# The last three experts of each layer: loads and products in the order gate, up, down of one expert

## What is computed

```python
def moe(h, router_w, router_b, w_gate, w_up, w_down):
    ...
    gates = jnp.sum(jax.nn.one_hot(idx, N_EXPERTS, dtype=jnp.float32) * w[..., None], axis=1)
    a = jnp.einsum("td,edf->tef", h, w_gate)
    u = jnp.einsum("td,edf->tef", h, w_up)
    z = jax.nn.silu(a) * u * gates[:, :, None].astype(h.dtype)
    return jnp.einsum("tef,efd->td", z, w_down)
```

```python
    h2 = rmsnorm(x, norm2_g) * (1 + scale2) + shift2
    x = x + gate2 * moe(h2.reshape(bsz * l, -1), router_w, router_b, w_gate, w_up, w_down).reshape(bsz, l, -1)
```

## Time and profile before

| | us |
|---|---|
| median of 3 runs | 1229.93 |
| lowest, highest | 1221.55, 1231.03 |
| profiled execution | 1229.87 |
| its span in the trace | 1228.2 |
| PE busy | 1109.6 (90%) |
| DVE busy | 558.6 (45%) |
| ACT busy | 355.9 (29%) |
| POOL busy | 234.7 (19%) |
| share of PE in the chain that ended last | 60% |
| share of DMA in that chain | 22% |

### The profile page before, as it was taken

The page is one execution under the profiler, slowest core; times in us unless marked ns, Lnnn a source line. Parts: engine busy times, 40 slices in busy tenths (PEclk is TensorE's granted clock), DMA queues, the critical chain, the costliest instruction groups (busy, mean ns, idle before and its releaser), DMA issues.

```text
span 1228.2 us, 18292 instructions
## 1 busy us (share of the span) xinstructions
PE 1109.6 (90%) x6948; PEld 520.5 (42%) x6948; DVE 558.6 (45%) x1342; ACT 355.9 (29%) x661; POOL 234.7 (19%) x339
## 2 busy tenths in 40 slices
PE   3999999899999987898899999998997999888886
PEld 1545556454443332333244655554544333232332
DVE  1275666743463332323265747666155433223327
ACT  2223445532323221221131424453223322221212
POOL 1222273411010111101020324541200011011100
PEclk9999889889989999999899998997998999899998
DMA  9939731656499999999790412046716799999995
GB/s 364 317 137 170 127 115 58 229 206 274 176 361 379 396 390 407 398 401 401 313 361 18 146 69 83 21 175 250 291 69 249 270 391 397 396 403 407 395 388 189
DMA packets 51214, 325.09 MB, mean 265 GB/s; under 512 B 6710, under 2 KB 7126, under 8 KB 32576
## 3 DMA queue, kind: packets, MB, share of 16 engines
q1 hardware_dynamic: 39296, 293.16, 61.1%
q0 software_dynamic: 10560, 26.17, 8.5%
q10 hardware_dynamic: 1280, 4.72, 0.9%
HBM read 316.15 MB, written 22.25 MB: 276 GB/s over the span
## 4 chain that ended last, share of the span: by engine, by line
PE 60%; DMA 22%; DVE 12%; issue 3%; ACT 2%; SPq 1%; DVEq 0%; ACTq 0%; POOLq 0%
PE ps L2216 19%; DMA ring<-moe_w_up 18%; PE ps L1828 14%; PE ps L1903 7%; PE ps L2106 7%; PE ps L1844 3%; DMA ring<-ada_w 3%; DVE attT L1318 2%; PE ps L1867 2%; PE ps L2000 2%; PE ps L2029 2%; DVE dbuf L1294 1%; PE ps L2205 1%; PE ps L1862 1%; DVE small L1427 1%
## 5 line engine op out<-in xcount | busy, mean ns | idle before, releaser
L2216 PE MATMUL ps<-ring,dbuf 128*32 128x512 f32 x2432 | 421.9, 605 | 35.0 <-DMA ring<-moe_w_up 23.5
L2216 PE MATMUL ps<-extra,dbuf 128*32 128x512 f32 x1312 | 248.9, 624 | 14.3 <-DMA ring<-moe_w_up 13.5
L2216 PEld LDWEIGHTS ps<-ring,dbuf 128*32 128x32 f32 x2432 | 115.3, 111 | 231.2 <-issue 220.6
L1828 PE MATMUL ps<-ring,extra 128*128 128x512 f32 (+1 forms) x384 | 150.6, 552 | 0.0
L1604 DVE COPY dbuf<-ps 128x256 f32<-128x256 f32 (+1 forms) x32 | 15.4, 483 | 212.3 <-PE ps L2205 212.3
L1903 PE MATMUL ps<-extra,ring 128*128 128x384 f32 x320 | 110.1, 503 | 0.0
L2216 PEld LDWEIGHTS ps<-extra,dbuf 128*32 128x32 f32 x1312 | 68.7, 114 | 89.5 <-issue 76.3
L866 POOL DMA_INDIRECT expert_rows<-big,lst x28 | 26.3, 940 | 409.6 <-DVE big L1626 205.2
L1828 PEld LDWEIGHTS ps<-ring,extra 128*128 128x128 f32 x384 | 74.3, 195 | 70.2 <-issue 66.7
L2106 PE MATMUL ps<-ring,extra 128*128 128x512 f32 x192 | 84.3, 594 | 3.0 <-DVE extra L1493 1.8
L1903 PEld LDWEIGHTS ps<-extra,ring 128*128 128x128 f32 x320 | 62.2, 197 | 42.7 <-issue 4.9
(11 more groups left out here) (310 smaller groups left out, 1452.9 us busy)
## 6 DMA issues: line engine op xcount, KB each, us to landing
extra<-moe_w_gate SPq DMA_DIRECT2D x32, 2048.0 KB, 17.3
ring<-moe_w_up SPq DMA_DIRECT2D x32, 2048.0 KB, 23.3
ring<-moe_w_down SPq DMA_DIRECT2D x30, 2048.0 KB, 22.3
ring<-ada_w SPq DMA_DIRECT2D x24, 2048.0 KB, 8.7
ring<-w_in SPq DMA_DIRECT2D x12, 2048.0 KB, 19.9
ring<-w_out SPq DMA_DIRECT2D x4, 2048.0 KB, 7.8
extra<-moe_w_down SPq DMA_DIRECT2D x2, 2048.0 KB, 15.9
skew_rows<-rpb_pad POOLq DMA_DIRECT2D x1, 3810.0 KB, 66.9
```

The costliest lines, as they stand in the source:

```text
L1828: ins = pe.matmul(out, a, b, start=(n == 0), stop=(n == len(pairs) - 1))
L2216: return pe.matmul(p[QT * g:QT * (g + 1), :], a, w, start=start, stop=stop, tile_position=(0, QT * g))
```

## The change

The last seven places of the load queue become down 13, gate 14, up 14, down 14, gate 15, up 15, down 15. On TensorE, experts 12 and 13 keep the old body; then `own_down(1)` runs the down product of 13 at once, and experts 14 and 15 (`alone=True`) run gate/up, and right behind it their own down product. `last_products` goes. On VectorE the scaling of expert 13's rows moves ahead of expert 14, the gate rows of 14 and 15 and the first `late_rows` move ahead of expert 15's product, and one `added` moves ahead of the second `late_rows`. The diagonal products run first, and the six `"cm"` products behind them; `keep_running(2)` goes. POOL's load of the final gain waits for the last gate/up product, since its slot now holds gate 14.

```diff
-            if q == 3 * NE - 1:
-                return "dn1", NE - 1
+            if q >= 3 * NE - 7:
+                return (("dn1", NE - 3), ("a", NE - 2), ("u", NE - 2), ("dn1", NE - 2), ("a", NE - 1), ("u", NE - 1), ("dn1", NE - 1))[q - 3 * NE + 7]
...
                 if l == L - 1:
+                    ready(pool, ("a", l), NE - 1)
                     pool.dma_start(fin, final_norm_g.partition_broadcast(P)).then_inc(d_fin, 16)
...
-                for e in range(EXP_PER_BODY):
-                    expert(NBODY - 1, e, next_=(e < EXP_PER_BODY - 1))
-                expert(NBODY, 0, last=True, next_=False)
+                expert(NBODY - 1, 0)
+                expert(NBODY - 1, 1)
+                products_out(NE - 3, SMALL)
+                for e in (2, 3):
+                    expert(NBODY - 1, e, next_=(e == 2), alone=True)
+                    products_out(NE - EXP_PER_BODY + e, SMALL)
+                act.activation(rneg[:, 0, :], eps, ACT.Sqrt)
...
-                for e in range(EXP_PER_BODY):
-                    expert(NBODY - 1, e, next_=(e < EXP_PER_BODY - 1))
+                expert(NBODY - 1, 0)
+                expert(NBODY - 1, 1)
+                rows_out(NBODY - 1, 1)
+                expert(NBODY - 1, 2, alone=True)
+                for j in range(LATE):
+                    gate_rows_of(NBODY - 1, EXP_PER_BODY - LATE + j, gate_rows[1], crossed=(j == 1))
                 if AHEAD[l]:
                     scales(l + 1, 0)
-                for j in range(LATE):
-                    gate_rows_of(NBODY - 1, EXP_PER_BODY - LATE + j, gate_rows[1], crossed=(j == 1))
                 late_rows(0)
+                expert(NBODY - 1, 3, next_=False, alone=True)
                 added(0, 0)
                 added(0, 1)
+                added(1, 0)
                 late_rows(1)
-                added(1, 0)
                 added(1, 1)
+                added(2, 0)
                 completed(0)
-                added(2, 0)
                 completed(1)
                 completed(2)
...
-                            if f == FC // 2 and not last and not next_:
-                                turn_products(es)
...
+                def own_down(es):
+
+                    e, blk = NE - EXP_PER_BODY + es, ("expert", l, queue_place("dn1", NE - EXP_PER_BODY + es))
+                    moved(pe, *product_of(l, NBODY - 1, es))
+                    turn("zt", e, [zb[0:CAP, f * P:(f + 1) * P] for f in range(FC)])
+                    pe.wait_ge(landed[SLOT_OF[blk]], 16 * NTH[blk])
+                    w = slot_of(SLOT_OF[blk]).rearrange("p (k n) -> p k n", k=FC)
+                    moved(pe, ("zt", l), e)
+                    job = (("dnz", l), 0) if e == NE - 1 else (("dn0", l), e)
+                    p = begin(pe, *job)
+                    for f in range(FC):
+                        for g in range(4):
+                            third, b = g % 2, g // 2
+                            ins = quarter(p, g, products_turned(SMALL)[:, f, QT * third:QT * (third + 1)], w[:, f, b * 512:(b + 1) * 512],
+                                          f == 0, f == FC - 1)
+                    fill(ins, *job)
...
-                for e in range(EXP_PER_BODY):
-                    expert(NBODY - 1, e, next_=(e < EXP_PER_BODY - 1))
-                expert(NBODY, 0, last=True, next_=False)
-                keep_running(2)
+                expert(NBODY - 1, 0)
+                expert(NBODY - 1, 1)
+                own_down(1)
+                for e in (2, 3):
+                    expert(NBODY - 1, e, next_=(e == 2), alone=True)
+                    own_down(e)
+                for n, (t, k) in enumerate(PE_PICKS):
+                    pe.wait_ge(d_yr[t][k], 16 * (l + 1))
+                    for b in range(2):
+                        pe.matmul(begin(pe, ("cm", l, t, b)), pick_diag[:, n, :], yr[k][:, t, b * 512:(b + 1) * 512], start=True, stop=False)
                 pe.wait_ge(s_fold, l + 1)
```

More of the change, by code:

```diff
@@ L1129, in expert @@
+                    if not first and not alone:
+                        products_out(e - 1, cap_of(i, es - 1))
                     if next_:
                         turned_out(e + 1, (es + 1) % 2, cap_of(i, es + 1))
-                    if not last and cap_of(i, es) == CAP:
+                    if cap_of(i, es) == CAP:
                         p = ready(act, ("u", l), use_of("u", i, es))
                         act.activation(by_chunk(sU)[0:2 * QT], in_rows(p)[2 * QT:P], ACT.Copy).then_inc(s_half, 1)
-                    if not first and next_ and cap_of(i, es - 1) == CAP:
+                    if not first and not alone and cap_of(i, es - 1) == CAP:
@@ L1626, in rows_out, with expert @@
                         release(dve, dve.tensor_tensor(y[0:SMALL, 512:D], p[SMALL:P], g[SMALL:P, 512:D], ALU.mult), ("dn0", l), e)
-                def expert(i, es, first=False, next_=True):
+                def expert(i, es, first=False, next_=True, alone=False):
                     e = i * EXP_PER_BODY + es
@@ L1652, in expert @@
                                                               op0=ALU.mult, op1=ALU.mult), ("u", l), n_u)
-                    if not first and next_:
+                    if not first and not alone:
                         rows_out(i, es - 1)
@@ L2216, in quarter, with expert @@
                     return pe.matmul(p[QT * g:QT * (g + 1), :], a, w, start=start, stop=stop, tile_position=(0, QT * g))
-                def expert(i, es, first=False, last=False, next_=True):
+                def expert(i, es, first=False, next_=True, alone=False):
                     e = i * EXP_PER_BODY + es
@@ L2250, in turn_products @@
                         turn("zt", i * EXP_PER_BODY + es, [zb[0:CAP, f * P:(f + 1) * P] for f in range(FC)])
-                    if not first and not last:
+                    if not first and not alone:
                         turn_products(es - 1)
@@ L2255, in expert @@
                         turn_rows(i, es + 1)
-                    if not last and large:
+                    if large:
                         n_u = use_of("u", i, es)
@@ L2277, in expert @@
                         fill(ins, *job)
-                    if not first and before_large:
+                    if not first and not alone and before_large:
                         n_dn = use_of("dn1", i, es - 1)
```

77 lines of the change are left out of this document (31 added, 46 removed).

## The result

| | before | after |
|---|---|---|
| median, us | 1229.95 (10 runs) | 1236.3 (10 runs, 1228.1 to 1238.75) |
| profiled execution, us | 1229.87 | 1236.45 |
| its span, us | 1228.2 | 1234.6 |
| PE busy | 1109.6 (90%) | 1100.3 (89%) |
| DVE busy | 558.6 (45%) | 557.7 (45%) |

The ratio of after to before is 1.0046, 95% interval 1.0024 to 1.0067: the change costs 5.7 us (3.0 to 8.2). The forecast was 3.1. The two profiled executions lie 6.6 us apart.

A forecast was written before the change was run, and what follows sets the result against it. The prediction took the in-order stream of expert weights, through the up-weight loads, to bound both expert parts. It summed 1229.87 us + 1.8 (first layer) + 1.3 (second) = 1233.0 us; this case's own range was 1226 to 1238.

The forecast's parts named there:

- Order of loads: Load queue, both layers: landing places are dealt out anew, so up weights of 14 and 15 land 5 us later.
- The stream did not catch up: Rival on weight loads: up weights of 14 and 15 land at their old times, 1222.6 us; chance 0.12.
- d13 costs nothing: TensorE: expert 13's down product, 3.62 us, fits into idle time before expert 14's up weights land; nothing lost.
- Clock of a14: TensorE, expert 14's gate/up product: 8.77 us taken, between 7.11 at full clock and 9.99; total 1231.5 to 1235.4 us.
- Own down product: TensorE, experts 14 and 15: 6.9 us from gate/up product's end to down product's end, the latter taking 3.62.
- The clock rival: TensorE's clock falls in the new bubbles: 3.6 us more per down product, four of them, 1247 us; chance 0.11.
- The sum: Expert part of each layer, up to x done: +1.8 us in the first layer, +1.3 us in the second.
- It reaches the end undiminished: After the first layer: its +1.8 us carries through, since TensorE's own work follows without waits for weights.
- VectorE's moved work: VectorE's end: some 5.8 us less behind expert 15's gated product; without it the end about 4.5 us later.
- Rows of 13 and reload: Store and reload of expert 13's rows: issued 11 us earlier, queued behind the last weights, landed by 1211; gain 0.24 us.
- the reload mixes with the weights: Rival: reload served beside the last weights, expert 15's up weights up to 5 us later per layer, 1242 us; chance 0.05.
- Diagonal products: TensorE's end, second layer: they run from 1212.1 to 1214.0, late-row products to 1219.3, with 0.6 us to spare.

The follow-up runs named there:

- e9: The changed kernel run once more without any edit; measured 1234.97 us, ratio 1.0043 to before.
- e1: The changed kernel with two unread filler matmuls between expert 15's gate/up product and the transposes of its products, in both layers; 1231.73 us, ratio 1.0007.
- e3: The changed kernel with the load order of before, keeping the new order of products; 1239.0 us, ratio 1.0119, from four runs.
- e10: The changed kernel with two unread filler matmuls ahead of expert 15's transposes, run a second time; 1232.2 us, ratio 1.0040.
- e6: The changed kernel with VectorE's gate rows, late rows and additions in the order of before; 1238.59 us, ratio 1.0083.
- e5: The changed kernel with the reload of stored rows held back until expert 15's gate/up product is done; 1246.8 us, ratio 1.0141.

## Why the prediction was right, and where its sizes were off

The sign and the mechanism were right: slower by a part of a per cent, because u14 and u15 land one place later and a bubble stands where the down product of before gave cover. The size was short: 3.1 us forecast, 5.7 (3.0 to 8.2) measured, so the forecast lies at the very edge of the interval. Two terms were short, d15's clock and u15's landing, and both on the same side. Step by step:

**Order of loads.** Second layer: the expert part starts 2.8 us later in this profile (955.81 against 952.98), so 1182.2 becomes 1185.0 for u14 and 1197.3 becomes 1200.1 for u15. They landed 0.25 us ahead of a14 and a15: at 1185.5 and 1201.25. The first layer's starts 0.6 us earlier (359.87 against 360.42), so 591.0 and 605.9 become 590.4 and 605.3, and they landed at 591.9 and 607.70. Short by 0.5 and 1.5 us for u14, by 1.2 and 2.4 us for u15: between them lie three places of 5.25 us, where my landing times had 5.03 and 4.97. The stream did not catch up.

**d13 costs nothing.** Right in after: it ends at 1183.64, 2.1 us before a14 can start.

**Clock of a14.** I took 8.77 us. In after's profile it was 7.07 in both layers, in e9's 8.77 and 8.43, in e1's 9.48 and 8.59: it goes on being either, as before. It mattered little: in after a15 then waits 1.76 us for u15, which is the case of the prediction's lower bound (+0.9 and +0.7 us); in e9, after a slow a14, a15 doesn't wait.

**Own down product.** 6.9 us were predicted from the end of a gate/up product to the end of its down product. For d14 of the second layer it is 1199.73 - 1192.80 = 6.93. For d15 it is 1217.14 - 1208.56 = 8.58. **This is the term that was mis-sized:** "I take this value for d14 and d15 of both layers" needs 3.62 us for d15, and it measured 5.34 in both layers of after, 4.87 on average over ten. The bubble ahead of d15 had the length foretold (3.24 us between the last matmul of a15 and the first of d15, predicted 3.3); what was left out of the likeliest case is that TensorE is slowed behind it more often than not, in 7 of 10 cases, by 1.15 to 2.66 us. The row that I took for evidence of full clock behind a bubble, the 3.62 us at 1204.93, had no bubble in front of it. TensorE's timeline of before has the other half of d14 there, right up to it:

```profile
1203.19 1.92 PE L2216 MATMUL ps<-ring,dbuf 128*32 128x512 f32 x16
```

d14 took 3.64 us in both layers of after, and in all products with its own order only 2 of 14 (e3 and e10) were slow, by 1.7 us.

The clock rival was priced at 3.6 us for each of four, with 0.11. It came in part: for one of the two products in most layers, and with a third to three quarters of that price, because only a part of a product runs at the lower level (granted clock 0.77 in the stretch of after shown above). All or nothing was the wrong way to cut it; the mean loss of 1.23 us at d15 alone would have put the forecast at 1235.5.

The Trainium skill (TensorE: Matmul & The Clock Gate, HAM oscillation — how this bites in real kernels), whose rule I had set against the row at 568.92, was the better guide for d15 (7 of 10 slow) and the worse for d14 (2 of 14). The case that all four are slow, 1247 us, came in no run.

**The sum.** x was done 4.4 us later in the first layer (predicted 1.8), of which 1.7 are d15's clock, and in the second layer's own part 3.6 us later (predicted 1.3), of which 1.7 again. In this profile a14 ran at full clock in both layers, so the prediction's figures for it are +0.9 and +0.7. The layers' parts are longer by 5.0 and 3.6; less 1.7 each for d15's clock, 2.4 and 1.2 are left over those figures, and u15's landing is late by just that. With d15's excess taken out, after, e9, e1 and e10 give +3.3, +1.6, +2.5, +3.6 in the first layer (mean 2.8) and +1.9, +1.4, +1.3, +0.7 in the second (mean 1.3). The second layer's sum stands; the first is short by about 1 us. In after that is u15's landing; in e10 u14 landed 2.1 us later behind the layer's first product than I had it, and in e1 a14 took 9.48 us for the 8.77 of the sum. Together 4.1 and 2.5 for d15 make 6.6 us, against 5.7 (3.0 to 8.2) measured.

**It reaches the end undiminished.** Of the 4.4 us at x, 2.8 are left at the second layer's first expert product. The other profiles vary by as much between these two points (323.1 to 325.3 us in eleven of twelve, 325.2 in before, 323.6 in after), so whether some of the delay is taken up there stays open.

**VectorE's moved work.** "Without them the end would be later by about the 4.5 us": e6 shows 3.7 us per layer where d15 is at full clock, 1.3 where it is slow, 2.3 in the times. The claim was an upper bound. x done 8.6 us after d15's end: measured 8.66.

**Rows of 13 and reload.** Issued at 600.5 and 1194.4. In the second layer that is 0.6 us late, with the shift of 2.8 (predicted 1191); in the first 3.5 us (predicted 597), since d13 ended at 590.08 and not 586.5, behind an a13 that ran partly at the lower clock in this profile. The second layer's first block landed behind d15's weights, the last one at 1197.0 + 17.3 = 1214.3, 0.5 us late with the shift and ahead of the diagonal products (1217.07). VectorE waits for no reloaded row. By the sign that the prediction set (u15 later than 607) the first layer's 607.70 would mean that the reload mixes with the weights. It doesn't: in e5, where the reload is issued only behind u15's landing, u15 lands 15.2 and 15.4 us behind u14; with the early reload it is 15.8 twice in after, and 15.0 and 15.3 in both e9 and e1. In after the long steps between them (5.5 us to d14, 5.3 to a15) were over, or nearly, when the reload was issued, at 1194.39, and the step to u15, with the reload queued, was 4.95. That the gain is 0.24 us was right as a saving of before; e5 shows that the new order leans on it.

**Diagonal products.** They fit behind d15 as predicted, and the six late-row products are each there in time: completed runs 4.45 us without a gap.

## To carry to other kernels

A product that runs between another one and the step that waits for its result gives cover twice: for the time until the data is there, and for the clock. When a reorder makes TensorE wait out a chain through two other engines, put an average clock loss on the product behind it, not zero and not the full price (here 1.23 us on d15, 0.24 on d14, where 3.6 was the price of all of it), and see whether matmuls that nobody reads fit into the wait. Before a row is used as evidence that a gap does no harm, look whether it has a gap in front of it. Moving a transfer forward in a full queue pays for itself only if somebody waited for that transfer; here each place forward moved the load that was waited for one place back.

## What the runs showed that I had not expected

Bubbles with nearly the same waits (2.13 to 2.17 us idle, transposes, 0.52 idle) end in down products of 3.64, 4.8, 5.34 or 6.3 us. In five of the ten the transposes already take longer than 0.55 us, so that there the clock fell inside the bubble. The bubble ahead of d14 (0.88 us of transposes, 1.35 idle, 0.55 of transposes, 0.58 idle; in e3 a wait for the weights more) is as long in sum and left 12 of 14 at full clock. Two matmuls of 1.98 us together in the longer idle part kept d15 at full clock 4 times in 4. Why one such bubble is followed by a fall and another is not stays open. The bubble alone doesn't settle it: the same wait of 2.16 us went both ways in e9.
